# Embedding LayerNorm of a hybrid attention layer: first tile scaled in halves, third tile's statistics moved behind the first gains, one filler in place of six

## The reference

```
h    = concat(meta, x)                                  # 528 rows of 1024
h    = (h - mean) * rsqrt(var + 1e-5) * ln_emb_g + ln_emb_b
proj = h @ w_in                                         # split into 11 parts
branch A: indexer scores -> top 128 keys per query -> softmax attention with T5 bias, 8 heads
branch B: low-rank q and kv (RMS norm, rotary key) -> causal softmax attention, 8 heads
out  = LN(2**0.25 * h + concat(oA*silu(ga), oB*silu(gb)) @ w_out)
```

## Time and profile before

| | us |
|---|---|
| median of 3 runs (328.76 to 329.11) | 329.11 |
| the profiled execution, its own time | 329.34 |
| its span, first to last instruction | 327.5 |
| PE busy in the span | 317.7 (97%) |
| DVE busy | 236.4 (72%) |
| POOL busy | 195.9 (60%) |
| ACT busy | 173.1 (53%) |

### The profile page before, as it was taken

How to read it: one execution, slowest core, us unless ns; L and a number is a source line. 1 busy time by engine, 2 the same in 40 slices (tenths; PEclk the granted TensorE clock), 3 DMA queues, 4 the chain that set the end, 5 groups by cost and what they waited for, 6 DMA issues and landing times.

```text
span 327.5 us, 6250 instructions
## 1 busy us (share of the span) xinstructions
PE 317.7 (97%) x2134; PEld 276.7 (84%) x2134; DVE 236.4 (72%) x630; ACT 173.1 (53%) x389; POOL 195.9 (60%) x243
## 2 busy tenths in 40 slices
PE   8999999999999999999999999999999999999991
PEld 7799987878778888987988988898978898998991
DVE  6984810279955799989995987478787866564786
ACT  4876843362442456367454764777586752822230
POOL 6552999989322261439440898889869582570222
PEclk9999999999999999999999999999999999999998
DMA  7664343249322122202300052322223111140033
GB/s 241 227 214 167 130 130 121 76 138 307 112 111 77 59 75 77 80 3 80 131 8 10 14 179 102 123 76 81 89 91 97 65 29 40 65 130 0 2 128 128
DMA packets 11997, 32.86 MB, mean 100 GB/s; under 512 B 2440, under 2 KB 2824, under 8 KB 11968
## 3 DMA queue, kind: packets, MB, share of 16 engines
q1 hardware_dynamic: 9232, 26.89, 24.0%
q10 hardware_dynamic: 2736, 5.59, 5.5%
HBM read 29.83 MB, written 4.81 MB: 106 GB/s over the span
## 4 chain that ended last, share of the span: by engine, by line
PE 93%; DVE 3%; DMA 2%; SPq 1%; issue 0%; DVEq 0%; ACT 0%
PE ps_j L1488 56%; PE ps_t L1488 8%; PE ps_o L1725 6%; PE ps_s L1676 6%; PE ps_s L1680 3%; PE ps_s L1649 3%; PE ps_t L1695 2%; PE ps_j L1542 2%; PE ps_t L1700 2%; DMA res<-in_x 2%; PE ps_j L1565 1%; PE ps_j L1443 1%; PE ps_j L1433 1%; DVE st L1039 1%; PE ps_j L1426 1%; PE ps_t L1702 1%
## 5 line engine op out<-in xcount | busy, mean ns | idle before, releaser
L590 POOL TENSOR_TENSOR wl<-raw,wh 128x1024 fp32r<-128x1024 f32 (+2 forms) x33 | 78.0, 2372 | 45.0 <-ACT wh L597 44.8
L1488 PE MATMUL ps_j<-hh,wh 128*128 128x512 f32 (+2 forms) x208 | 72.9, 350 | 0.0
L1488 PE MATMUL ps_j<-hl,wh 128*128 128x512 f32 (+2 forms) x208 | 72.4, 348 | 0.0
L1488 PE MATMUL ps_j<-hh,wl 128*128 128x512 f32 (+2 forms) x208 | 72.1, 347 | 0.0
L750 POOL TENSOR_SCALAR pr<-pr,rden 128x528 f32<-128x528 f32 (+1 forms) x64 | 34.7, 560 | 50.0 <-DVE rden L1301 50.0
L991 ACT ACTIVATE pr<-pr,mn 128x528 f32<-128x528 f32 (+1 forms) x64 | 36.0, 564 | 15.6 <-DVE mn L1290 15.6
L1488 PEld LDWEIGHTS ps_j<-hh,wh 128*128 128x128 f32 (+1 forms) x208 | 38.8, 186 | 5.9
L1488 PEld LDWEIGHTS ps_j<-hh,wl 128*128 128x128 f32 (+1 forms) x208 | 38.8, 187 | 5.1
L1488 PEld LDWEIGHTS ps_j<-hl,wh 128*128 128x128 f32 (+1 forms) x208 | 38.7, 186 | 5.0
L597 ACT ACTIVATE wh<-raw 128x1024 fp32r<-128x1024 f32 (+2 forms) x34 | 34.9, 1039 | 0.2 <-DMA raw<-in_weights 0.2
L768 POOL TENSOR_TENSOR bm<-bias,mask 128x144 f32<-128x144 f32 (+3 forms) x32 | 27.4, 890 | 1.4 <-DVE mask L1272 1.4
(11 more groups left out here) (287 smaller groups left out, 844.4 us busy)
## 6 DMA issues: line engine op xcount, KB each, us to landing
raw<-in_weights SPq DMA_DIRECT2D x35, 512.0 KB, 3.3
bias_by_distance<-bias_vector ACTq DMA_DIRECT2D x1, 2624.0 KB, 13.1
bias<-bias_by_distance ACTq DMA_DIRECT2D x8, 264.0 KB, 2.7
res<-in_x SPq DMA_DIRECT2D x4, 512.0 KB, 4.8
out<-res SPq DMA_DIRECT2D x3, 512.0 KB, 2.6
raw<-in_weights SPq DMA_DIRECT2D x5, 256.0 KB, 6.3
pt<-in_ln_emb_g SPq DMA_DIRECT2D x1, 512.0 KB, 5.5
pt<-in_ln_emb_b SPq DMA_DIRECT2D x1, 512.0 KB, 6.2
```

Source lines behind the costliest of these rows:

```text
L590: eng.tensor_tensor(ring_of(False, b), raw_of(b), ring_of(True, b).bitcast(F32), ALU.subtract).then_inc(done, 1)
L1488: last = pe.matmul(dst, a, b, start=n == 0 and part[0], stop=n == count - 1 and part[1])
```

## The change

On ACT, the first tile is scaled by a new function `first_tile` in two halves of 512 columns, with the square root of the second tile between them; `high(1)` and `gains_of(2)` now stand ahead of the square root of the third tile. On DVE, both statistics of the third tile stand behind `gains_of(1)`, those of the fourth behind `low(1)`, and the reciprocal of the third behind `gains_of(3)`. On PE, one filler stands in place of six, the waits on `xn_act` count the additional half, `low(2)` stands ahead of the wait for the third and fourth tile, and `low(3)` ahead of `spread(6)`.

```diff
--- before.py
+++ after.py
@@ -808,6 +808,12 @@
                 act.activation(src, src, ACT.Identity, bias=nmr[0:r, t:t + 1],
                                scale=rstd[0:r, t:t + 1]).then_inc(xn_act, 1)
 
+            def first_tile(half):
+
+                src = res[:, 0, 512 * half:512 * half + 512]
+                act.wait_ge(shift, 4)
+                act.activation(src, src, ACT.Identity, bias=nmr[:, 0:1], scale=rstd[:, 0:1]).then_inc(xn_act, 1)
+
             def gains_of(u):
 
                 act.wait_ge(x_t, u + 2)
@@ -829,17 +835,18 @@
             deviation(0)
             normal(0, 2)
             deviation(1)
-            normal(1, 4)
+            first_tile(0)
             deviation(2)
+            first_tile(1)
             act.wait_ge(first_in[0], 16)
             act.activation(wh[:, 0:4, 0:P], raw[:, 0, 0:4, :], ACT.Copy).then_inc(w_first_act, 1)
             act.wait_ge(par_in, 32)
             gains_of(0)
             high(0)
+            high(1)
+            gains_of(2)
             deviation(3)
             negative(3)
-            high(1)
-            gains_of(2)
             high(2)
             normal(3, 6)
             deviation(4)
@@ -1080,21 +1087,21 @@
             stat(2, 0)
             inverse(1, 3)
             stat(2, 1)
-            stat(3, 0)
             inverse(2, 5)
-            stat(3, 1)
             dve.wait_ge(first_in[1], 16)
             dve.tensor_copy(wh[:, 0:4, P:2 * P], raw[:, 1, 0:4, :]).then_inc(w_high_dve, 1)
             dve.wait_ge(par_in, 32)
             gains_of(1)
-            stat(4, 0)
-            inverse(3, 6)
-            stat(4, 1)
+            stat(3, 0)
+            stat(3, 1)
             low(0)
             gains_of(3)
+            inverse(3, 6)
             low(1)
+            stat(4, 0)
+            stat(4, 1)
+            low(2)
             inverse(4, 7)
-            low(2)
             low(3)
 
             pm = ps_t[:, 0:P].rearrange("p (c n) -> p c n", c=DC)
@@ -1445,11 +1452,12 @@
                     if u == DC - 1:
                         last.then_inc(job_mm, 1)
 
-            busy(6)
+            busy(1)
             pe.wait_ge(xn_act, 2)
             pe.wait_ge(xn_dve, 1)
             spread(0)
             spread(1)
+            pe.wait_ge(xn_act, 3)
             pe.wait_ge(xn_dve, 2)
             spread(2)
             spread(3)
@@ -1458,12 +1466,12 @@
             low(0)
             high(2, 1)
             high(3)
-            pe.wait_ge(xn_act, 4)
+            low(2)
+            pe.wait_ge(xn_act, 5)
             spread(4)
             spread(5)
-            low(2)
+            low(3)
             spread(6)
-            low(3)
             spread(7)
             high(4)
             low(4)
```

## The result

| | before | after |
|---|---|---|
| median | 329.11 us (328.76 to 329.86, 7 runs) | 330.34 us (330.01 to 330.62, 7 runs) |
| profiled execution, its own time | 329.34 us | 330.03 us |
| its span | 327.5 us | 328.2 us |
| PE busy | 317.7 us | 316.5 us |

The medians differ by 1.23 us. The ratio after to before is 1.0032 with a 95% interval of 1.0022 to 1.0042, which is 1.1 us (0.7 to 1.4). The forecast was 329.95, slower.

A forecast was written before the change was run, and what follows sets the result against it. PE was taken as the bound, with 93% of the time and full from 27 us on, so only the first job's start counts. Net 0.85 us later: 329.11 + 0.85 = 329.96, given as 329.95; range 328.8 to 330.6.

The forecast's parts named there:

- Part 1: First tile in halves on ACT, one filler on PE: a half 0.77 us, `spread(0)` at about 9.59, 0.55 earlier.
- The rule that I cited: Skill page's price of an ACT instruction: about 0.3 us plus 0.83 ns an element, so 0.72 us for a half.
- Parts 2 and 3: DVE without the third tile's statistics: weight block 1 rounded at 10.77, low part of unit 1 ending at 15.74, 0.25 earlier.
- first rival: Weight block 1's transfer lands earlier in timed executions, gains of unit 1 at 10.62: only 0.41 later, 329.5; 22 in 100.
- Part 4: Fourth tile's statistics behind unit 1's low part on DVE: aggregate at 17.19, ACT's high part of unit 3 at 18.07.
- Part 5: PE idle 1.2 us at unit 3's high pass, `spread(4)` at 19.62, unit 4's high pass at 21.99: net 0.85 later.
- The sum: Whole kernel: net 0.85 us later, 330.19 for a profiled execution, 329.95 for the median.
- The second: x tiles land later in timed executions, where the old order would wait: at 1.5 us late, 328.7, faster; 10 in 100.
- The fourth: PE doesn't wait at unit 3, as something on DVE or ACT is shorter in the new order: 328.85; 10 in 100.
- The third: PE's idle 1.2 us and missing fillers lower TensorE's clock, costing 2.6 us: 332.6; 4 in 100.

The follow-up runs named there:

- all but the halves: The changed kernel with the first tile scaled whole and six fillers again: 330.38 us, ratio 1.0039.
- four-filler kernel: The kernel before with the first tile scaled in halves around the square root and four fillers: 328.92 us, ratio 0.9992.

## Why the prediction was right

**Part 1** held in its numbers: `spread(0)` at 9.58 for 9.59, the high pass of unit 0 at 12.08 for 12.06, a half at 0.81 for 0.77. (The Trainium skill, "ScalarE: Activation LUTs", section "What ACT_TABLE_LOAD costs", puts an ACTIVATE at 186 ns, 0.833 ns an element and some 93 ns for each pointer operand. With bias and scale as pointers that is an estimate of 0.80 us for 512 columns, and this trace agrees. The rule that I cited counts one pointer.) That six fillers hold the first spread is true of one of the three traces with six fillers, the one that I had, whose start was slow; in the kernel with all but the halves it comes at 9.87 and waits for data. The start at 9.59 was so in part luck.

**Parts 2 and 3** were right in kind, DVE idle until the transfer is there and the same work behind it, and the size was off: 0.30 us of idle time, ended at 10.17 and not 10.74. That landing is the first rival's, which let the gains of unit 1 start behind `spread(1)` and gave 0.41 us for the whole. The trace of after has its condition and its path, at 10.76 for the rival's 10.62, but its time did not come: 0.69 between the traces, 1.2 between the medians. The landing gives 0.3 us at DVE (gains at 10.76 for 11.06), as `spread(1)` doesn't let more through, and this is the distance of all later numbers of mine from the measured ones: low part of unit 1 at 15.45 for 15.74, aggregate at 16.89 for 17.19, unit 3's high part at 17.79 for 18.07.

**Part 4** gave the wait and the place exactly, and its cause in part. ACT's 0.59 us for the aggregate was in it; the 0.66 us for the third tile's reciprocal, longer still, was not written down, since it is hidden behind the longer wait as long as the fourth tile's aggregate comes last. The experiments put the cause ahead of where I had it, and don't isolate it. With the third tile's statistics left where they are, the fourth's could not stand earlier without loss (330.67). A part of what was given away is the time ahead of weight block 1: an instruction there is free (330.24), and with the third tile's statistics there 0.6 to 0.75 us come back (329.59). But with the fourth's back as well the loss is 1.1 us again (330.22), with two waits on ACT that my part 4 didn't have, for DVE's gains of unit 1 and for the third tile's reciprocal. So what the change does besides moving statistics away, the later root and reciprocals, which I had not priced, is enough to lose most of it again, with the third tile's first statistics behind the second tile's reciprocal (0.31 us at DVE's rounding). How the loss divides among them and the moved statistics stays open.

**Part 5** held: idle 1.22 for 1.2 us, `spread(4)` at 19.43 for 19.62, the high pass of unit 4 at 21.83 for 21.99. Its side remark that the moved low pass hides 0.5 us was wrong; taking it back cost nothing in the median (330.23) and 0.16 us by the two traces.

**The sum** was 0.85 us against 0.69 between the two traces and 1.2 (0.7 to 1.4) between the medians. That the forecast of the median came within 0.4 us has luck in it: the sum was 0.16 too high for the traces, and the step from a trace to the median, which I took as a constant 0.23 us, is +0.23 for the one trace and -0.31 for the other; over the fourteen traces here it runs from -0.33 to +1.13.

**The rivals.** The second (late x tiles) isn't borne out: the loss is there in all timed executions. Such a landing exists, though: in the profiled execution of the four-filler kernel DVE stood 0.96 us for the third tile, and it took 1.13 us more than its median. The fourth fell with PE's 1.22 us. The third, the clock, did not happen in the changed kernel's 7 executions, but a lower mean clock showed in four of six with 1.81 us of idle time, and in one trace the clock fell behind 0.30 us and a single filler, as the rival's words on missing fillers have it. I had read the earlier trace rows as asking for a much longer idle time; that reading was wrong.

## What to carry to other kernels

Before a piece of work is moved out of an engine's wait for a transfer, count what the engine has to do behind that wait: work inside it is free as far as the wait lasts (0.3 us for the transfer and 0.2 for PE here), and the same work behind it may not be. And a strict queue passes a delay on: ask for every instruction that will now wait what stands behind it on the same engine, here the high part of a unit behind a square root. Where an effect of 0.3% is at stake, a pair of traces is good for the mechanism and uncertain for the size: a single execution lay up to 0.3 us below and 1.1 us above its median here. Line two traces up by an early event, such as the first spread, before their later times are compared. And an edit that "puts a thing back" shows its cause only if the old order is restored exactly.

## What was not expected of the hardware

An idle time of PE of 1.81 us, with 0.17 us three us ahead of it, was followed in the traced execution by some 3 us at a granted clock of 0.50, which began only about 1 us after PE was busy again. A lower mean clock showed in four of six executions, so that kernel has two times, 1 to 2 us apart. In another kernel 0.30 us of idle time behind a single filler were followed, 0.2 us after PE was busy again, by some 3 us at 0.50, in one traced execution; its 1.22 us of idle time were not. With 1.1 to 1.2 us of idle time a low mean clock showed in 3 executions of 36, of which that is one.

The same transfer, the same place in the same queue, landed at 10.75 in one execution and at 10.17 in another, and in that of the four-filler kernel 7.0 us after its issue, at about 11.45. The 30 fillers at the start took 6.18 us in one execution of the kernel before and 5.03 in another.
